# Routed expert rows: gated on the way out of PSUM and added to the residual in memory by the scatter, and a last norm that runs tile by tile

## The reference, cut to what matters

```python
h = rmsnorm(x, norm_ffn_g[l])
x = x + hierarchical_moe(h, w_group[l], w_expert[l], w1[l], w3[l], w2[l])
return rmsnorm(x, final_norm_g)

# in hierarchical_moe: each token picks 1 of 4 groups and 2 of the 8 experts in it
gate = grp_p * (top_p / jnp.sum(top_p, axis=-1, keepdims=True))
hid = jax.nn.silu(xblk @ w1[eid]) * (xblk @ w3[eid])      # expert: 1024 -> 512
yb = hid @ w2[eid]                                        # 512 -> 1024
y = jnp.zeros((N, D), h.dtype).at[row_tok].add(yb * row_gate[:, None].astype(yb.dtype))
```

## Time and profile before

| | |
|---|---|
| median of three runs | 2121.28 us |
| profiled execution | 2119.76 us, span 2118.0 us, mean granted clock 0.971 |
| PE busy | 1997.0 us (94%) |
| DVE busy | 1131.6 us (53%) |
| ACT busy | 947.2 us (45%) |
| POOL busy | 274.6 us (13%) |
| chain that ended last, by engine | PE 80%, DVE 7%, issue 5%, DMA 3%, ACT 2% |
| DMA | 413.44 MB, mean 195 GB/s; 376 to 386 GB/s in the ten slices that hold most of the expert blocks |
| idle of ACT before `yb` (L1314) | 125.4 us in 64 instructions, 104.4 of it put down to the scatter's landing |

### The profile page before, as it was taken

How to read it: one execution, slowest core, us unless ns; L and a number is a source line. 1 busy time by engine, 2 the same in 40 slices (tenths; PEclk the granted TensorE clock), 3 DMA queues, 4 the chain that set the end, 5 groups by cost and what they waited for, 6 DMA issues and landing times.

```text
span 2118.0 us, 27570 instructions
## 1 busy us (share of the span) xinstructions
PE 1997.0 (94%) x10406; PEld 1695.6 (80%) x10406; DVE 1131.6 (53%) x1348; ACT 947.2 (45%) x1317; POOL 274.6 (13%) x372
## 2 busy tenths in 40 slices
PE   7999999999999999997999999998999999999970
PEld 7988888888888888887898787886788888888860
DVE  5106642112132323124677677346888888888857
ACT  5223222223344333312346344113777777777742
POOL 0000000022323231100000000000131222222210
PEclk9999999999999999999999999997999999999985
DMA  4211224253435354234224463326999999999936
GB/s 174 98 44 60 80 80 159 91 175 107 164 135 168 134 173 138 105 140 171 89 72 141 162 243 120 133 81 219 355 376 378 378 380 381 384 386 380 367 141 248
DMA packets 131256, 413.44 MB, mean 195 GB/s; under 512 B 16528, under 2 KB 37728, under 8 KB 125277
## 3 DMA queue, kind: packets, MB, share of 16 engines
q1 hardware_dynamic: 107180, 351.90, 44.5%
q0 software_dynamic: 23984, 60.26, 8.5%
HBM read 351.05 MB, written 77.82 MB: 202 GB/s over the span
## 4 chain that ended last, share of the span: by engine, by line
PE 80%; DVE 7%; issue 5%; DMA 3%; ACT 2%; POOLq 0%; POOL 0%; ACTq 0%; DVEq 0%; SPq 0%
PE psum L620 22%; PE psum L622 22%; PE psum L621 22%; PE psum L2292 2%; PE psum L2277 2%; PE psum L2183 1%; PE psum L2161 1%; DMA expert_rows<-yb,aidx 1%; DVE e_l L1969 1%; PE psum L2512 1%; PE psum L2169 1%; PE psum L2436 1%; PE psum L2132 1%; PE psum L2238 1%; PE psum L2533 1%
## 5 line engine op out<-in xcount | busy, mean ns | idle before, releaser
L1969 DVE TENSOR_TENSOR e_l<-e_raw,e_h 128x2048 fp32r<-128x2048 f32 x190 | 424.1, 2285 | 33.8 <-ACT e_h L1292 33.6
L620 PE MATMUL psum<-hT_h,w_l 128*128 128x512 f32 x1088 | 431.9, 397 | 0.0
L622 PE MATMUL psum<-hT_h,w_h 128*128 128x512 f32 x1088 | 424.3, 390 | 0.0
L621 PE MATMUL psum<-hT_l,w_h 128*128 128x512 f32 x1088 | 423.7, 389 | 0.0
L1292 ACT CAST e_h<-e_raw 128x2048 fp32r<-128x2048 f32 x190 | 353.1, 1932 | 22.1 <-PE psum L622 11.5
L1400 DVE TENSOR_TENSOR w_l<-wraw,w_h 128x2048 fp32r<-128x2048 f32 (+1 forms) x38 | 87.0, 2290 | 287.6 <-ACT w_h L986 287.6
L622 PEld LDWEIGHTS psum<-hT_h,w_h 128*128 128x128 f32 x1088 | 204.2, 188 | 43.7
L621 PEld LDWEIGHTS psum<-hT_l,w_h 128*128 128x128 f32 x1088 | 204.6, 188 | 40.1
L620 PEld LDWEIGHTS psum<-hT_h,w_l 128*128 128x128 f32 x1088 | 204.5, 188 | 39.7
L620 PE MATMUL psum<-e_h,xT_l 128*128 128x512 f32 x512 | 204.3, 399 | 8.2 <-DVE e_l L1969 4.7
L621 PE MATMUL psum<-e_l,xT_h 128*128 128x512 f32 x512 | 201.3, 393 | 0.0
(11 more groups left out here) (381 smaller groups left out, 3360.8 us busy)
## 6 DMA issues: line engine op xcount, KB each, us to landing
e_raw<-in_w_e SPq DMA_DIRECT2D x192, 1024.0 KB, 8.9
wraw<-in_w_in_t SPq DMA_DIRECT2D x37, 1024.0 KB, 4.8
pt_scratch<-stage SPq DMA_DIRECT2D x52, 512.0 KB, 2.6
gate<-pt_scratch SPq DMA_DIRECT2D x24, 512.0 KB, 3.6
rows<-rows_scratch SPq DMA_DIRECT2D x8, 1280.0 KB, 8.7
h_scratch<-xn SPq DMA_DIRECT2D x16, 512.0 KB, 3.6
yg<-expert_rows SPq DMA_DIRECT2D x8, 1024.0 KB, 12.8
c_all<-attention_scratch POOLq DMA_DIRECT2D x4, 1560.0 KB, 10.4
```

Source lines behind the costliest of these rows:

```text
L620: nc.tensor.matmul(out_ap, ll, rh, start=first, stop=False)
L621: nc.tensor.matmul(out_ap, lh, rl, start=False, stop=False)
L622: return nc.tensor.matmul(out_ap, lh, rh, start=False, stop=last)
L1969: nv.tensor_tensor(e_l[:, c], e_raw[:, c], e_h[:, c].bitcast(F32), ALU.subtract).then_inc(s_el13 if c < 4 else s_el2, 1)
```

## The change

- `h_scratch` (now `h2_scratch`) holds 1024 rows and each tile is stored once; the second store of `h2_stored` now writes x2's tile into a new `x3_scratch` (1024 rows). Row tables give the same number for a token's first and second choice.
- The gates are made before block 0's products: DVE `gate_exponents`, ACT two exponentials, DVE `gates_made`, PE `gate_table` (16 products, the same one-hots as the row table times gates), DVE `gates_read` into `rgate`. PE's seven unused products before the first rows become three. For the extra blocks `ohb_over` is twice as wide, and one more copy takes the gates out. The one-hots of the first group are kept (`ohp_first`), in the slot of `e_raw` chunk 5; `e_raw`'s slots are in the opposite order, and the first load of chunk 5 waits for the gate table.
- `rows_out` multiplies by the block's gate column `gcol` as it leaves PSUM; POOL moves that column after each scatter.
- The scatter goes to `x3_scratch` with an add: each row of `yb` is added to the row that lies in memory.
- At the end the meeting of the engines, the two loads per tile, the gates and the three DVE passes are gone. When the last scatter has landed, SP loads eight tiles of 512 KB back, and squares, root, refinement, scaling and store follow tile by tile.

```diff
-                for a in range(2):
-                    at = a * T + t * P
-                    sp.dma_start(h2s[at:at + P, :], xn2[:, t % 2]).then_inc(s_x2d[t % 2], 16)
+                sp.dma_start(h2s[t * P:(t + 1) * P, :], xn2[:, t % 2]).then_inc(s_x2d[t % 2], 16)
+                sp.dma_start(x3d[t * P:(t + 1) * P, :], x2[:, t]).then_inc(s_x2s, 16)
...
             for c in range(2, 6):
+                if c == 5:
+                    sp.wait_ge(s_rta, 4)
                 load_chunk(0, 0, c)
...
-            sp_phase_done(sp)
-
             sp.dma_start(gfin[:], g_fin).then_inc(s_fx, 16)
+            sp.wait_ge(s_all, 1)
             for t in range(NT):
-                sp.dma_start(yg[:, t], ybs.rearrange("(a t p) d -> t p a d", a=2, p=P)[t]).then_inc(s_fg[t], 16)
+                sp.dma_start(x3[:, t], x3d[t * P:(t + 1) * P, :]).then_inc(s_fg[t], 16)
...
-                pool.indirect_dma_start(out=ybs, out_offset=bass.IndirectOffsetOnAxis(ap=aidx[:], axis=0), in_=yb[:],
-                                        in_offset=None, bounds_check=last_row, oob_is_err=False).then_inc(s_ys, 16)
+                pool.indirect_dma_start(out=x3d, out_offset=bass.IndirectOffsetOnAxis(ap=aidx[:], axis=0), in_=yb[:],
+                                        in_offset=None, bounds_check=last_row, oob_is_err=False, compute_op=ALU.add).then_inc(s_ys, 16)
+                if last:
+                    return
+                pool.tensor_copy(gcol[:], rgate[:, bass.ds(b + 1, 1)]).then_inc(s_gc, 1)
...
             def rows_out(b, first):
+                act.wait_ge(s_gc, b + 1)
                 if not first:
                     act.wait_ge(s_ys, b * 16)
                 for r in range(2):
                     act.wait_ge(s_e2, b * 2 + 2)
-                    nc.scalar.copy(yb[:, r * HALF:(r + 1) * HALF], ps[4 + r]).then_inc(s_ye, 1)
+                    nc.scalar.activation(yb[:, r * HALF:(r + 1) * HALF], ps[4 + r], ACT.Copy, scale=gcol[:]).then_inc(s_ye, 1)
...
+            def x3_squares(t):
+                act.wait_ge(s_fg[t], 16)
+                if t:
+                    act.wait_ge(s_ss, t)
+                nc.scalar.activation(psum[:, 0:D], x3[:, t], ACT.Square, accum_out=ss[:, t:t + 1]).then_inc(s_ss, 1)
...
+            for t in range(NT):
+                x3_squares(t)
+                if t:
+                    x3_root(t - 1)
+            x3_root(NT - 1)
...
+            def gates_made():
+                dve.wait_ge(s_gx, 2)
...
+                r.link(nv.tensor_tensor(ohb[:], O[:], gates_of(NX), ALU.mult))
...
+            gate_exponents()
             low(0, 0)
+            gates_made()
             rows_low(0)
             low(0, 1)
+            gates_read()
             overflow_places()
...
             dve.wait_ge(s_fx, 16)
             for t in range(NT):
-                dve.wait_ge(s_fg[t], 16)
-                cd.link(nv.tensor_scalar(yg[:, t, 0], yg[:, t, 0], gates2[:, t, 0:1], None, ALU.mult))
-                cd.link(nv.scalar_tensor_tensor(yg[:, t, 0], yg[:, t, 1], gates2[:, t, 1:2], yg[:, t, 0], ALU.mult, ALU.add))
-                nv.tensor_tensor(x3[:, t], x3[:, t], yg[:, t, 0], ALU.add).then_inc(s_f3, 1)
-            inverse_rms(dve, 0)
-            for t in range(NT):
-                nv.scalar_tensor_tensor(x3[:, t], x3[:, t], rs[:, t:t + 1], gfin[:], ALU.mult, ALU.mult).then_inc(s_fo, 1)
+                x3_mean(t)
+                if t:
+                    x3_scaled(t - 1)
+            x3_scaled(NT - 1)
...
+            def gate_table():
+                pe.wait_ge(s_rd1, GATED)
...
-            unused_products(7, 4)
+            unused_products(3, 4)
+            gate_table()
```

More of the change, by code:

```diff
@@ L533, in build @@
         pz = rm("pz", [P, 1])
+        rgate = rm("rgate", [P, NX + N_OVER])
+        gcol = rm("gcol", [P, 1])
         E_AT = rm.at
-        e_raw = rm("e_raw", [P, 6, 4 * FF])
+        e_raw = rm("e_raw", [P, 6, 4 * FF])[:, ::-1]
+        ohp_first = Region(nc, E_AT)("r_ohp_first", [P, 6, P])
+        assert E_AT + 4 * 6 * P <= END_CONST
         e_h = rm("e_h", [P, 6, 4 * FF], F32R)
@@ L581, in build @@
         s_ys = sem("expert_rows_stored")
[L583 to L588, removed]
+        x3 = Region(nc, X2_AT)("x3", [P, NT, D])
+        gfin = Region(nc, X2_AT - 4 * D)("gfin", [P, D])
+        assert rm2.at <= X2_AT - 4 * D
+        s_fg = [sem(f"x3_loaded{t}") for t in range(NT)]
         s_fx = sem("final_gain_loaded")
-        s_f3 = sem("x3_made")
         s_fo = sem("output_made")
         s_out = sem("output_stored")
[L594 to L607, removed]
-            for t in range(NT):
[L609 to L614, removed]
         block = ctx.enter_context(nc.Block())
@@ L928, in next_gather, with store @@
                 gather(b, bidx[:])
-            def store(b, first=False):
+            def store(b, first=False, last=False):
                 if not first:
@@ L945, in _ @@
             next_gather(3)
+            pool.wait_ge(s_rd1, GATES_READ)
+            pool.tensor_copy(gcol[:], rgate[:, 0:1]).then_inc(s_gc, 1)
+            pool.wait_ge(s_x2s, 16 * NT)
             store(0, True)
@@ L950, in _ @@
             for b in range(NX - 3, NX):
-                store(b)
+                store(b, last=b == NX - 1)
             pool.wait_ge(s_rd1, OVER_READ)
@@ L958, in _ @@
                     pool.drain()
+                    pool.tensor_copy(gcol[:], rgate[:, bass.ds(b, 1)]).then_inc(s_gc, 1)
                     gather(b, aidx[:])
@@ L1313, in rows_out @@
                     act.wait_ge(s_e2, b * 2 + 2)
-                    nc.scalar.copy(yb[:, r * HALF:(r + 1) * HALF], ps[4 + r]).then_inc(s_ye, 1)
-            for c in range(4):
+                    nc.scalar.activation(yb[:, r * HALF:(r + 1) * HALF], ps[4 + r], ACT.Copy, scale=gcol[:]).then_inc(s_ye, 1)
+            for c in range(2):
+                high(0, c, True)
+            act.wait_ge(s_rd1, GATES_MOVED)
+            nc.scalar.activation(gd[:], gd[:], ACT.Exp).then_inc(s_gx, 1)
+            nc.scalar.activation(md[:], md[:], ACT.Exp).then_inc(s_gx, 1)
+            for c in range(2, 4):
                 high(0, c, True)
@@ L2465, in counts @@
                 mm(o, ones[:], Osum[:, NT - 1], start=False, stop=True).then_inc(s_cnt, 1)
+            def gate_table():
+                pe.wait_ge(s_rd1, GATED)
+                for n, (t0, t1) in enumerate(ROUTE_GROUPS):
+                    for a in range(2):
+                        for t in range(t0, t1):
+                            o = (ohp_first, ohp, ohp_last)[n]
+                            ins = mm(ps[7][:, 64:64 + NX], o[:, a * (t1 - t0) + t - t0], ohb[:, a, t],
+                                     start=n == 0 and a == 0 and t == t0, stop=n == 2 and a == 1 and t == t1 - 1)
+                ins.then_inc(s_rta, 1)
             def overflow_table():
```

98 lines of the change are left out of this document (59 added, 39 removed).

## The result

| | before | changed |
|---|---|---|
| median, us (runs) | 2120.9 (4) | 2147.01 (4; 2143.89 to 2150.01) |
| ratio, 95% interval | | 1.0133 [1.0100, 1.0166] |
| profiled span, us | 2118.0 | 2146.2 |
| one turn of POOL's loop, us | 18.17 | 20.27 |
| last scatter's issue to the end, us | 59.3 | 33.5 |

It is 1.3% slower; the forecast was 0.3% slower.

The account below looks back on a forecast made before the run. POOL's serial loop of DMA landings (18.18 us a turn) was taken to bound, just above PE's 17.81. Span 2118.0 - 22.3 (tail) + 0.5 (entry) + 27.6 (blocks) = 2123.8, time 2127.1 us (+0.3%); 8-in-10 range 2099 to 2180.

Parts of the forecast that it names:

- What bounds the loop: Expert blocks: POOL's serial gather and scatter landings set the pace, 18.18 us a turn, just above PE's 17.81.
- The scatter that adds: POOL's loop: the adding scatter lands later, lengthening each turn by 1.15 us; loss in the blocks 27.6 us.
- The 1.35: Scatter landing: extra 1.35 us, from doubling the last scatter's 9 slices of 0.15 us on the fullest engine.
- the equation: Loop turn: D = 1.35 - 0.097 x (5.1 D - 3.9), longer turns thinning weight loads and added reads raising the engines' share.
- D: As quantity: growth of a loop turn, forecast 1.15 us. As rival: tail gives less, 5 us at most; chance 0.03 including others.
- point of decision: Loop: at a turn longer by 0.93 us, the blocks lose what the tail gives.
- The lead of 2.3 us: Expert blocks: PE's remaining lead and POOL's early slack take 2.3 us off the loop's 29.9 us loss.
- The tail: After the last scatter: tile-by-tile tail paced by DVE at 2.25 us a tile, gain 22.3 us.
- The entry, gating, stores: Before and in the blocks: entry +0.5 us (0 to +4), gating in rows_out 0, stores of h2 and x2 0.
- A: Rival, scatter in the loop: the added read is hidden, turn growth under 0.5 us, 2099.5 to 2108 us; chance 0.25.
- B: Rival, loop: the DMA engines become the bound, at least 18.7 us a turn, 2113.5 us; chance 0.15.
- C: Rival, POOL's loop: old row fetched first, turn longer by 4 us or more, 2201 up to 2295 us; chance 0.12.

Follow-up runs that it names:

- e1: Changed kernel with plain scatters instead of adding ones (sum of rows left out): 2088.47 us, ratio 0.9842.
- e2: Kernel before, with its scatter made to add and x2 stored ahead as rows to add to: 2170.58 us, ratio 1.0236.
- e12: As e7, but the first of the two plain scatters cut to 64 bytes a row: 2135.6 us, ratio 1.0077.
- e11: Changed kernel, block 0's rows scattered again after the last store, plain and adding in turns: start to start 3.47 and 6.26 us at 4 KB.
- e3: Changed kernel, POOL's two loop drains replaced by a semaphore wait for the index copy: 2124.09 us, ratio 1.0023.
- e4: Kernel before, POOL's two loop drains replaced by a semaphore wait for the index copy: 2116.08 us, ratio 0.9983.
- e9: As e5, with the loop's two drains replaced by a semaphore wait for the index copy: 2106.6 us, ratio 0.9934.
- e7: As e1, but every plain scatter issued twice, into two different tensors: 2160.12 us, ratio 1.0207.
- e10: As e1, with three one-column POOL additions between the drain and the plain scatter: 2189.92 us, ratio 1.0333.
- e8: As e1, with three one-column POOL additions before the drain of each scatter: 2089.95 us, ratio 0.9898.
- e5: Changed kernel, scattering plainly into 2048 rows, x2 kept in SBUF, DVE adding a token's two rows in the tail: 2107.78 us, ratio 0.9948.

## Why the prediction was right or wrong

**What bounds the loop: right.** POOL's chain through both landings sets the turn, PE runs at full clock. The fixed 0.8 us behind each landing shows it in the traces, and e1, e2 and e12 move the turn by moving the landing.

**The scatter that adds: right in kind, the size failed.** The step was "If reading two rows for each one written doubles that, a scatter lands 1.35 us later". Alone, it lands 2.8 us later (e11): 0.52 us because POOL's issue lasts longer, which no term had, and 2.27 us of transfer against 1.35. The last scatters of the two kernels, the very row that the prediction went by, say the same: 3.2 and 6.2 us to landing, 0.98 and 1.56 us of issue, so 2.4 us more of transfer. In the loop the landing grew by 2.6 us, of which the issue is 1.04 (1.90 to 2.94 us from 1500 to 2000 us) and the rest 1.5. The turn grew by 2.10 us instead of 1.15. The 1.35 itself was read wrong: the line of the earlier trace rows has eight slices over zero, 1.20 us, and by that the equation gives D = 1.06.

Put into the equation, 2.8 in place of 1.35 gives D = (2.8 + 0.38) / 1.49 = 2.13. That it comes so near 2.10 is partly chance. With the issue as long as it is in the loop the extra would be 3.3 us and D 2.5, and the engines' share fell by 4.1 points, where the equation has 6.8 at this D. The Trainium skill's rule on reduces ("Collectives: The Full Stack", section "The bandwidth ceiling: the fold count and why AG ≠ RS ≠ AR") is a doubling as well; the 2.1 times of the loop are near it, the 2.7 to 2.9 times alone are not.

**The lead of 2.3 us: wrong in sum.** POOL's early turns grew at once (from the fifth gather to the sixth 20.62 us, 17.88 before), so 27 turns grew and not 26. PE did give up its lead at the end: its last transposes start 7.5 us after the last gather's issue, 9.0 before. But from there to the last scatter it took 41.4 us instead of 38.5, with ACT waiting up to 7.5 us for one of the last weight chunks, 5.5 before. 27 x 2.10 = 56.8, and 1.4 behind the last gather, against 27.6.

**The tail: right, 3.4 us small.** -25.7 against -22.3. From the first reload to the end it took 25.8 us (28.5 forecast): DVE had some 2.03 us of work a tile (2.25 forecast), 1.8 us in eight tiles, and the end came 3.4 us after the last scaling (4.4). The reloads began 0.75 us sooner behind the last scatter.

**The entry, gating, stores: right.** +0.4 us where +0.5 stood. ACT's gated copies cost nothing: e1 has them and runs at PE's pace.

**Outside the terms.** 4.6 us that the profiled run gained up to the first gather. That is chance: in the profiled executions of all kernels here the first gather starts anywhere from 1443.6 to 1449.2 us, in e1 and e3 at 1447.9 and 1449.2. Together: the loop cost 30.6 us more than forecast, tail and front gave 8.0 more, which is the 22.4 between +5.8 and +28.2 but for the entry.

**The rivals.** A (the read hidden) is excluded by the landing of 11.4 us. B is not there in the changed kernel, since the slower loop leaves the engines 5%; e3 shows it as the next bound, at 19.0 us a turn (18.7 was its price). C (D of 4 or more) is excluded, though its point of decision, D = 0.93, was passed by the forecast's own mechanism. D did not happen: the reloads began 7.8 us behind the last scatter's issue, 8.5 before.

## What to carry over

The accumulating scatter moved work from an engine to the DMA path at 2 to 3 times the engine time of a plain one and with a longer issue: before you use one, read whether its landing stands in a serial chain and whether the DMA engines are full. Here both held, and a sum that cost VectorE 19 us once in the tail cost 58 us in the loop. Price a new kind of DMA by one measured alone, since a loop multiplies the error of a guess by its turns. Where GpSimd waits for its own DMA in a drain although only a small copy must be finished, a semaphore on the copy lets two transfers overlap, if nothing else keeps them apart: in e4 they did, in e3, with the engines full, they did not.

## What the runs showed of the hardware

- A drain on GpSimd held until its indirect DMA had landed: the next indirect DMA was issued 0.8 us after each landing, in every turn. With a semaphore on the copy instead, the scatter was issued 2.7 (e4) and 2.4 us (e9) before the gather's landing.
- An adding scatter of 47 rows of 4 KB, alone, took 2.7 to 2.9 times the engine time of a plain one (22.2 to 23.6 against 8.2 engine-us) and landed 2.8 us later; in the loop it took 2.1 times as much, as did two plain ones (e11, e7).
- One-column GpSimd operations took up to 2.3 us instead of 0.2 beside VectorE's 2.2 us subtractions of two SBUF operands, 1.8 on average (e10, e8). The issue of an indirect DMA stretches too: 1.56 us alone and 2.81 on average in the changed kernel, 0.98 and about 1.8 for the plain one.
- Kernels whose GpSimd chain is almost as long as PE's turn spread widely: e8 in two groups 18 us apart, e5 from 2100 to 2120 us. The profiled ones had turns of 17.83 (e8, fast group) and 18.54 us (e5, slowest), so both paces occur; without the drains the spread was 5 us (e9). What tips a run one way was not found.
